# Last mixer: scores of two pairs side by side, and other places for turns, values, maxima, divisions and lower parts

## The reference

```python
qkv = h @ w_qkv
logit_own = einsum('bhqd,bhkd->bhqk', qf, k_own) * scale + bias_own
logit_own = where(dist_own >= 0, logit_own, -inf)
p = softmax(logit_own)
out = einsum('bhqk,bhkd->bhqd', p, v_own)
return out @ w_o
```

## Time and profile before

| | |
|---|---|
| median of 3 runs | 1143.5 us (1143.5 to 1143.5) |
| profiled execution, its time | 1144.46 us |
| profiled execution, its span | 1142.7 us |
| TensorE busy | 1119.2 us, 98% |
| VectorE busy | 831.1 us, 73% |
| ScalarE busy | 587.0 us, 51% |
| last mixer, chunks 4 to 14 | some 83 us, from 863 us on |

### The profile page before, as it was taken

The page is one execution under the profiler, slowest core; times in us unless marked ns, Lnnn a source line. Parts: engine busy times, 40 slices in busy tenths (PEclk is TensorE's granted clock), DMA queues, the critical chain, the costliest instruction groups (busy, mean ns, idle before and its releaser), DMA issues.

```text
span 1142.7 us, 15900 instructions
## 1 busy us (share of the span) xinstructions
PE 1119.2 (98%) x6253; PEld 929.6 (81%) x6253; DVE 831.1 (73%) x1368; ACT 587.0 (51%) x912; POOL 56.8 (5%) x105
## 2 busy tenths in 40 slices
PE   8999999999999999999999999999999998999997
PEld 7767568888878887888888878888879886888886
DVE  6569449878775777698788889877884557656664
ACT  7345445454445675645444674444466566544442
POOL 1101000000000000010000001000011000000000
PEclk9999999999999999999999999999999999999999
DMA  9526259987844334798876279778636443755530
GB/s 337 169 93 226 76 211 369 340 294 274 309 155 147 122 137 165 268 400 310 297 281 239 74 259 408 287 280 301 237 121 230 157 149 98 276 200 199 185 111 37
DMA packets 39578, 252.19 MB, mean 221 GB/s; under 512 B 6744, under 2 KB 6944, under 8 KB 10832
## 3 DMA queue, kind: packets, MB, share of 16 engines
q1 hardware_dynamic: 26928, 189.67, 46.3%
q0 software_dynamic: 12576, 61.51, 14.8%
HBM read 249.37 MB, written 4.25 MB: 222 GB/s over the span
## 4 chain that ended last, share of the span: by engine, by line
PE 87%; DVE 7%; ACT 3%; issue 1%; DMA 1%; POOL 0%; DVEq 0%; ACTq 0%
PE bank L1487 51%; PE bank L1638 25%; PE bank L1931 2%; PE bank L1690 2%; PE bank L1715 1%; PE bank L1753 1%; PE bank L1571 1%; DVE x L922 1%; PE bank L1912 1%; DMA u<-qk 1%; DVE work L920 1%; PE bank L2002 1%; DVE wlo L1051 1%; DVE wlo L899 1%; DVE us L966 0%
## 5 line engine op out<-in xcount | busy, mean ns | idle before, releaser
L899 DVE TENSOR_TENSOR wlo<-raw,whi 128x2048 fp32r<-128x2048 f32 x140 | 319.0, 2283 | 61.2 <-ACT whi L554 61.1
L554 ACT ACTIVATE whi<-raw 128x2048 fp32r<-128x2048 f32 x141 | 267.9, 1904 | 2.4 <-DMA raw<-in_stream 1.5
L1487 PE MATMUL bank<-whi,hh 128*128 128x512 f32 x544 | 214.1, 394 | 0.0
L1487 PE MATMUL bank<-wlo,hh 128*128 128x512 f32 x544 | 212.4, 390 | 0.0
L1487 PE MATMUL bank<-whi,hl 128*128 128x512 f32 x544 | 211.8, 389 | 0.0
L1638 PE MATMUL bank<-us,whi 128*128 128x512 f32 x832 | 197.0, 389 | 0.0
L1638 PEld LDWEIGHTS bank<-us,whi 128*128 128x128 f32 x832 | 156.2, 188 | 32.4
L1487 PE MATMUL bank<-us,whi 128*128 128x256 f32 x880 | 168.0, 291 | 0.0
L1487 PEld LDWEIGHTS bank<-us,whi 128*128 128x128 f32 x880 | 137.7, 192 | 9.0 <-issue 8.2
L1487 PE MATMUL bank<-whi,us 128*128 128x512 f32 (+2 forms) x384 | 122.2, 386 | 5.7 <-DVE us L966 1.6
L625 ACT ACTIVATE hh<-work 128x512 fp32r<-128x512 f32 x56 | 35.4, 633 | 173.3 <-PE bank L1487 173.3
(11 more groups left out here) (239 smaller groups left out, 1172.5 us busy)
## 6 DMA issues: line engine op xcount, KB each, us to landing
raw<-in_stream SPq DMA_DIRECT2D x176, 1024.0 KB, 4.9
qk<-in_w_mod POOLq DMA_DIRECT2D x48, 1024.0 KB, 5.6
bias_rows<-bias_heads POOLq DMA_DIRECT2D x4, 768.0 KB, 17.6
u<-bias_rows POOLq DMA_DIRECT2D x16, 128.0 KB, 2.9
vo<-feature_rows POOLq DMA_DIRECT2D x3, 512.0 KB, 8.8
raw<-in_stream SPq DMA_DIRECT2D x2, 696.0 KB, 8.0
x<-in_x SPq DMA_DIRECT2D x2, 512.0 KB, 4.7
cb<-feature_rows POOLq DMA_DIRECT2D x2, 512.0 KB, 6.6
```

The costliest lines, as they stand in the source:

```text
L554: nc.scalar.activation(whi[:, c % RING, 0:w], raw[:, n % RING, 0:w], ACT.Copy).then_inc(hi_ready, 1)
L899: nc.vector.tensor_tensor(wlo[:, c % RING, 0:w], raw[:, raw_index(c) % RING, 0:w], whi[:, c % RING, 0:w].bitcast(fp32), ALU.subtract).then ...
L1487: ins = mm(out, st, mv, start=start and i == 0, stop=stop and i == 2, skip_group_check=True)
```

## The change

Only three tables of the last mixer change. The same steps are issued, with the same code, at other places. The lines that are spoken of below, cut from the diff:

```diff
-B_PE = {"score": {0: (4, 2), 1: (5, 0), 2: (6, 1), 3: (7, 0), 4: (9, 0), 5: (10, 2), 6: (12, 1), 7: (12, 2)},
+B_PE = {"score": {0: (4, 1), 1: (4, 1), 2: (6, 1), 3: (6, 1), 4: (8, 2), 5: (8, 2), 6: (12, 1), 7: (12, 1)},
...
-        "upper": {0: (7, 0), 1: (9, 0), 2: (12, 3), 3: (15, 0)}}
-B_DVE = {"max": {0: (4, 2), 1: (5, 0), 2: (6, 0), 3: (6, 3), 4: (8, 2), 5: (10, 0), 6: (12, 0), 7: (12, 2)},
-        "lower": {0: (6, 3), 1: (8, 0), 2: (13, 3), 3: (15, 3)},
...
+        "upper": {0: (7, 3), 1: (10, 0), 2: (13, 0), 3: (15, 3)}}
+B_DVE = {"max": {0: (3, 1), 1: (4, 2), 2: (6, 0), 3: (6, 3), 4: (7, 2), 5: (9, 2), 6: (12, 1), 7: (12, 2)},
+        "lower": {0: (7, 0), 1: (11, 2), 2: (13, 1), 3: (15, 0)},
```

More of the change, by code:

```diff
@@ L112 @@
         "scale": {0: (7, 0), 1: (10, 0), 2: (11, 3), 3: (14, 2)}}
-B_PE = {"score": {0: (4, 2), 1: (5, 0), 2: (6, 1), 3: (7, 0), 4: (9, 0), 5: (10, 2), 6: (12, 1), 7: (12, 2)},
[L114 to L119, removed]
-        "upper": {0: (7, 0), 1: (9, 0), 2: (12, 3), 3: (15, 0)}}
-B_DVE = {"max": {0: (4, 2), 1: (5, 0), 2: (6, 0), 3: (6, 3), 4: (8, 2), 5: (10, 0), 6: (12, 0), 7: (12, 2)},
-        "lower": {0: (6, 3), 1: (8, 0), 2: (13, 3), 3: (15, 3)},
-        "divide": {0: (5, 0), 1: (6, 0), 2: (6, 2), 3: (7, 2), 4: (9, 0), 5: (10, 1), 6: (12, 3), 7: (13, 0)}}
+B_PE = {"score": {0: (4, 1), 1: (4, 1), 2: (6, 1), 3: (6, 1), 4: (8, 2), 5: (8, 2), 6: (12, 1), 7: (12, 1)},
+        "turn": {0: (5, 0), 1: (5, 3), 2: (6, 1), 3: (6, 2), 4: (7, 2), 5: (7, 3), 6: (8, 1), 7: (8, 3), 8: (9, 2), 9:
+            (10, 1), 10: (11, 3), 11: (12, 0), 12: (13, 0), 13: (13, 2), 14: (13, 3), 15: (14, 1)},
+        "value": {0: (6, 1), 1: (7, 1), 2: (8, 2), 3: (9, 2), 4: (11, 2), 5: (12, 1), 6: (13, 3), 7: (14, 2)}}
+B_ACT = {"exps": {0: (4, 0), 1: (5, 3), 2: (6, 1), 3: (6, 2), 4: (8, 1), 5: (10, 0), 6: (12, 2), 7: (12, 3)},
+        "copy": {0: (5, 0), 1: (6, 0), 2: (6, 1), 3: (6, 3), 4: (6, 3), 5: (7, 1), 6: (8, 0), 7: (8, 1), 8: (9, 1), 9:
+            (11, 1), 10: (11, 2), 11: (12, 1), 12: (13, 1), 13: (13, 3), 14: (14, 1), 15: (14, 2)},
+        "upper": {0: (7, 3), 1: (10, 0), 2: (13, 0), 3: (15, 3)}}
+B_DVE = {"max": {0: (3, 1), 1: (4, 2), 2: (6, 0), 3: (6, 3), 4: (7, 2), 5: (9, 2), 6: (12, 1), 7: (12, 2)},
+        "lower": {0: (7, 0), 1: (11, 2), 2: (13, 1), 3: (15, 0)},
+        "divide": {0: (4, 0), 1: (5, 2), 2: (7, 0), 3: (7, 0), 4: (8, 3), 5: (10, 3), 6: (12, 3), 7: (13, 2)}}
 QUARTERS = tuple((i, u) for i in range(16) for u in range(4))
```

## The result

| | before | changed |
|---|---|---|
| median, 20 runs of each | 1143.5 us | 1144.06 us |
| lowest of these | 1139.19 us | 1143.56 us |
| profiled execution, time | 1144.46 us | 1143.64 us |
| profiled execution, span | 1142.7 us | 1141.8 us |
| ratio | | 1.0024, 95% interval 1.0013 to 1.0034 |

The changed kernel is slower by 0.24%, between 0.13 and 0.34%. The three runs of before that were shown ahead all stood at 1143.5 us. In 20 runs the kernel before has two groups: 7 runs up to 1140.9 us and one at 1141.7, and 12 from 1143.5 to 1145.4 us. The changed kernel has 18 from 1143.56 to 1146.5 us and two at 1148.5 and 1149.7. The lowest times are 4.4 us apart, the medians 0.6.

The account below looks back on a forecast made before the run. TensorE's own instructions were taken to bound the last mixer. Doubled scores +5.0, edges -0.2 and the last lower part -0.5 us gave +4.3 us, so the median 1143.5 becomes 1147.8 us; range 1146.3 to 1150.8 us.

Parts of the forecast that it names:

- doubled place: Two pairs' scores side by side in the last mixer: TensorE idle 1.45 us, net 1.25 us each, +5.0 us for four.
- The wait at chunk 15: TensorE's 0.46 us wait at project chunk 15 for the last lower part would go: -0.46 us.
- Edges: Steps side by side among the mixer's weight products share an edge, 0.20 us less than apart; balance -0.2 us.
- the lower part: Lower part 3 moves to (15, 0) on VectorE, ready 1.3 us before chunk 15 wants it: -0.46 us.
- The sum, +4.3 us: All terms in the last mixer: +5.0 - 0.2 - 0.5 us; this forecast had a chance of 0.62.
- VectorE's wait at maxima 0: VectorE stands from 855.7 to 865.7 us for the first scores; 3 us of cover before chunk 5, cost nothing.
- the forecast's own bound: Whole time: a measurement can tell 0.2%, 2.3 us; slower above 1145.8 us had 0.93, same 0.05, faster 0.02.
- a rival about the change: TensorE's clock falls around doubled places: 1149.5 us with one fall, 1154.6 with four; chance 0.15 for one or more.
- The wait is cheaper: At doubled places, second scores begin before both maxima are read, or the 0.96 us overlaps; some 1146 us, chance 0.08.
- One more thing is late: In the mixer a copy or lower part misses its place, or VectorE is not free; 1149 to 1151 us, chance 0.12.
- Not slower: Edges between products and steps limit the mixer, steps at 22 places instead of 26; 1143.0 us, chance 0.03.

Follow-up runs that it names:

- third experiment: Changed kernel with the second pair of scores at each of the four places one quarter later; 1140.25 us, ratio to the kernel before 0.9996.
- second profile of before: The kernel before, unchanged, run and profiled again; 1140.89 us over 12 runs, ratio 1.0003.
- second profile of the changed kernel: The changed kernel, unchanged, run and profiled again; the profiled execution took 1148.10 us, the 11 runs 1144.22 us, ratio 1.0033 to the kernel before.

## Why the prediction was right and wrong

**Right: the bound, the mechanism and the sum of the change.** TensorE bounds the mixer, and each doubled place makes it wait for the maxima. Start to start was forecast at 2.30 us from three rows and is 2.30 us at all four places; one place alone costs 1.24 us (forecast 1.25); taking the four apart again gives back 4.97 us (forecast 5.0). The wait at chunk 15 is gone from the changed kernel. Edges and the lower part together give 0.8 us in the third experiment (forecast 0.7; the edges' share of it was not measured alone). The sum, +4.3 us, is 4.2 us in the stretch. VectorE's wait at maxima 0, 10.0 us, cost nothing, and no copy or lower part was late in the way that the rival had it: TensorE has no wait in the stretch but those four and the norm's 0.50 us.

**Wrong: the level on which the sum was put.** The failed step is the last one: "The median of the runs, 1143.5, is 1.0 us below the profiled time and becomes 1147.8 us". I took three equal times and a profile near them as the kernel's time. They were from the upper group, 4.3 us above the lowest run, and the profiled execution had lost 4.9 us ahead of the mixer. Where the three lost their time is not on record, since none was profiled. Over all 109 runs of the kernel before the median is 1140.06 us and 34 are above 1143.4; over 31 runs of the changed kernel it is 1144.21 us, and 6 are above 1147. The difference of the medians, 4.15 us or 0.36%, is close to the forecast of 4.3 us. Within the lower groups alone it is 4.1 us (1139.83 to 1143.93). The level that the sum belongs on is the lower one: 1139.8 + 4.3 gives 1144.1 us, and 1144.06 was measured.

That the median of before came out at 1143.5 us in 20 runs as well, and the ratio at 0.24% only, fits chance in the draw: 12 of those 20 runs are in the upper group, against 22 of the other 89, and 2 of the 20 of the changed kernel, against 4 of its other 11. By the forecast's own bound (slower above 1145.8 us) the measured median is "same", which had a chance of 0.05.

The profile had given a warning. I used, a fall of the clock that cost 1.7 us behind an idle time of 2.52 us, only for a rival about the change, and did not ask whether every execution has it. The idle time goes back to VectorE's late start on a transferred tile; in the second profile of before that wait is 0.2 us. The mean clock of 0.995 is by itself no measure of luck, since the second profile has 0.998: the difference, 0.003 of the span, is 3.4 us. A range for a time has to hold the spread of the base as well: from the lowest level that the profile allows (1144.5 less at most 5.7 us: an estimate from 2.2 us of the transfer, 1.7 us of the clock at 53 us and the 1.8 us that a granted share of 0.91 means over the 20 us from 630 on) to 1143.5.

**The rivals.** The clock did not fall at the doubled places: 1.00 throughout in both profiles of the changed kernel. It did fall at 53 us in the first profile of before, behind 2.52 us of idle time, and between 636 and 641 us in several profiles, with no idle time ahead. By the rule of the Trainium skill ("TensorE: Matmul & The Clock Gate", Part 1: The HAM clock gate), an array that was idle is given half the clock. The trace agrees at 53 us; the waits of 1.38 us did not bring a fall about, and the falls from 636 us on had no idle time ahead. "The wait is cheaper" (some 1146 us, +0.22%) is near the measured ratio by its number, but not by its reason: the waits are as long as forecast. "One more thing is late" did not come about. "Not slower" fell: it needed a wait below 0.2 us net, and one doubled place costs 1.24 us.

## What to carry to other kernels

Two steps that use the same buffer must stand at least as far apart in the waiting engine's queue as the reading of the first takes; here 2.3 us from start to start. The scores and one quarter of a chunk behind them take 2.48 us and cover it; side by side nothing does. Before a sum is put on a measured time, ask which parts of that execution are luck: late transfers, waits behind them, and stretches with a lower granted clock. And compare two profiles from a common event on, not by their spans: the spans here said 0.9 us faster, the stretch 4.2 us slower.

## What the runs showed of the hardware

TensorE's clock fell in some executions in a stretch with no idle time in its row, between 636 and 641 us (16 products of one row by 16 columns ahead of it, then products of 128 and of 16 columns). In the second profile of the changed kernel it stayed at 1.2 GHz for some 10 us, to 648 us, though full products had come back by 642.6 us; in other executions of the same kernel it did not fall at all. In the profiles with four and with eight full products of 0.23 us among the small ones it fell too (0.50 from 640 to 642 us in both). Four waits of 1.38 us within 70 us did not lower it in either profile of the changed kernel.
